# Input projection of a hybrid decoder layer by pairs of column tiles, seven products for eight

## The chip, the core and the metric

The kernel runs on one core of a Trainium2 chip. The metric is the device time of one execution in microseconds (us); lower is better. The engines are PE (TensorE: matmuls), DVE (VectorE), ACT (ScalarE), POOL (GpSimd) and SP, which here only issues DMAs. Each engine runs its own instructions in order, and semaphores order the engines against each other.

## The reference

One step of a one-layer decoder trunk on 512 prompt positions and 64 sample positions (8 sequences of 8), model width 2048. The 576 positions are the moving columns of every large matmul.

```python
h = rmsnorm(x, norm_mix_g)
p = h @ w_in                        # 2048 x 5120: [u_A | v_A | B_gate | C_gate | x_B], 1024 columns each
u = gelu(p[..., :o1])
v = rmsnorm(gelu(p[..., o1:o2]), sgu_norm_g)
bg, cg, xb = p[..., o2:o3], p[..., o3:o4], p[..., o4:]
y_a = u * chunk_sgu(v, w_s, b_s)    # per head: causal 128x128 mixing of positions, plus a bias
zc, new_mix = causal_dwconv(cg * xb, mix_prev, conv_mix_w, conv_mix_b)   # 3 taps
y_b = bg * zc
y = concat(group_rmsnorm(y_a, ..., 8), group_rmsnorm(y_b, ..., 8))       # 16 heads of 128 channels
x = x + y @ w_out
h = rmsnorm(x, norm_ffn_g)
gate, new_ffn = causal_dwconv(h @ w_gate, ffn_prev, ...)
x = x + (silu(gate) * (h @ w_up)) @ w_down
y_out = rmsnorm(x, final_norm_g)
```

## The kernel before

**Data and products.** Everything is held transposed: channels on the 128 partitions, the 576 positions along the free dimension, in two halves of 288 (`HALF`). Float32 accuracy comes from splitting each operand into a high and a low float32r part and making three matmuls: `hi*hi`, `hi*lo`, `lo*hi` (`three`, L1980 to L1982). ACT makes the high part of a weight piece (`w_hi`, L801), DVE subtracts to make the low part (`w_lo`, L1317). A piece is 128x1024 values, half of the rows of one 128-column tile, loaded by SP into one of the two buffers of `raw`. Four pieces fit in `w_hi` and `w_lo`.

**Input projection.** `w_in` has 40 column tiles. One tile is `gemm`: 16 row blocks x 3 matmuls x 2 halves = 96 matmuls of 128x128 by 128x288. The first two tiles run together with the start of the program; the others follow in loops: 8 tiles of v, 8 of u, then 8 times x, C gate, B gate (`group_b`).

**Start.** SP loads x in five blocks (`x_nat`: four of 128 positions, one of 64). PE transposes four 128x128 blocks at a time against the identity (a unit; L2045), DVE multiplies a unit by the norm's gain (L1354), ACT makes `h_hi` (L838) and keeps a copy in `X` (L853), DVE makes `h_lo` (L1343). The norm's own factor is not known yet: the squares are summed beside the first matmuls (ACT L844, DVE L1366), their inverse roots are spread over the partitions by PE (L2059), and every tile of the projection is multiplied by them as it leaves PSUM (`times_rb`, L1326).

**Heads.** While PE runs the u tiles, v is normalised, transposed and mixed per head. Each of the 16 heads of y is squared, split, summed over its 128 channels by PE (`y_ssq`, with a 128x128 block of ones), rooted by ACT (L828), inverted by DVE (L1331, 128x576) and multiplied in place in `X`, one head after the other between the tiles.

**Output projection and the rest.** The first two tiles of `w_out` run row block by row block as the heads of y are ready (`gemm2_by_k`); the residual x comes back from DRAM (`xT_scratch`) by four DMAs of POOL (L623). From the feed-forward part on, pairs of column tiles are made in seven products for eight (Strassen's scheme in Winograd's form: 168 matmuls of 288 columns for 192), with DVE forming sums of weight quadrants (L1685 to L1698) and ACT and DVE combining the results out of PSUM. ACT and DVE run ahead of PE by a four-slot ring of `w_hi` and `w_lo`: piece q may be split once product q-4 is done.

## Time and profile before

| | us |
|---|---|
| median of 3 runs (lowest to highest) | 2291.45 (2290.77 to 2295.84) |
| span of the profiled execution, first to last instruction | 2290.3 |
| PE busy | 2255.6 (98%) |
| DVE busy | 1670.7 (73%) |
| ACT busy | 1021.1 (45%) |
| POOL busy | 498.6 (22%) |
| granted TensorE clock, mean of the span | 0.996 |

Only the span is recorded of the profiled execution, no time of its own; the median of the runs is 1.15 us above it. Busy time of PE counts matmuls whose spans overlap, so that its rate is better read from counts of matmuls over a stretch.

### The profile page before, as it was taken

The page shows a single profiled execution, that of the slowest core. Times are in us where ns is not written, and L with a number is a line of the kernel's source. Part 1 is how long each engine was busy: PE and PEld are TensorE (multiplying, and loading weights), DVE is VectorE, ACT ScalarE, POOL GpSimd, SP SyncE. Part 2 cuts the span into 40 slices and gives each one's busy share as a digit, 9 for nine tenths or more (in the row PEclk, how much of TensorE's full clock was granted, in tenths as well). Part 3 has the DMA queues.
Part 4 walks back from the last instruction along what each step waited for, and adds up shares of the span by engine and source line. Part 5 has one row for each costly group of instructions (what it writes and reads, how often), then busy time and mean ns, then how long its engine had stood idle before and what let it go on. Part 6 is the DMA issues. An engine that isn't in the chain of part 4 may idle for free.

```text
span 2290.3 us, 44103 instructions
## 1 busy us (share of the span) xinstructions
PE 2255.6 (98%) x16946; PEld 2244.7 (98%) x16946; DVE 1670.7 (73%) x2265; ACT 1021.1 (45%) x1608; POOL 498.6 (22%) x593
## 2 busy tenths in 40 slices
PE   7999999999999999999999999999999999999997
PEld 7999999999999999999999999999999999999997
DVE  6347754545522698888888888888888798888886
ACT  6234321212211355455454444545444565555565
POOL 2310000000222011111111111111112356655573
PEclk9999999999999999999999999999999999999998
DMA  7322222232533245454444435344445566765433
GB/s 244 98 76 75 75 82 86 73 92 83 187 101 110 71 116 156 128 163 127 144 140 136 150 121 166 125 146 138 138 150 209 194 228 220 232 228 193 168 113 110
DMA packets 369510, 320.05 MB, mean 140 GB/s; under 512 B 8712, under 2 KB 348803, under 8 KB 364160
## 3 DMA queue, kind: packets, MB, share of 16 engines
q1 hardware_dynamic: 346608, 203.98, 30.5%
q0 software_dynamic: 22800, 114.69, 13.6%
q8 instruction: 66, 1.08, 0.2%
q14 instruction: 36, 0.29, 0.0%
HBM read 258.32 MB, written 60.31 MB: 139 GB/s over the span
## 4 chain that ended last, share of the span: by engine, by line
PE 59%; DMA 1%; DVE 1%; POOL 0%; issue 0%; ACT 0%; POOLq 0%; ACTq 0%
PE ps L2301 13%; PE ps L2303 13%; PE ps L2302 13%; PE ps L2362 6%; PE ps L2364 6%; PE ps L2363 6%; DMA down<-in_w_down_dram 1%; DMA form<-act_scratch 1%; PE ps L2376 0%; DVE dw_lo L1828 0%; DVE w_lo L1672 0%; PE ps L2420 0%; PE ps L2422 0%; PE ps L2421 0%; POOL down_s L714 0%
## 5 line engine op out<-in xcount | busy, mean ns | idle before, releaser
L1980 PE MATMUL ps<-h_hi,w_hi 128*128 128x288 f32 x1728 | 512.9, 297 | 0.0
L1982 PE MATMUL ps<-h_hi,w_lo 128*128 128x288 f32 x1728 | 509.2, 295 | 0.0
L1981 PE MATMUL ps<-h_lo,w_hi 128*128 128x288 f32 x1728 | 509.1, 295 | 0.0
L2362 PE MATMUL ps<-form,dw_hi 128*128 128x288 f32 x1204 | 357.3, 297 | 4.2 <-issue 1.7
L2363 PE MATMUL ps<-form,dw_hi 128*128 128x288 f32 x1204 | 354.3, 294 | 0.0
L2364 PE MATMUL ps<-form,dw_lo 128*128 128x288 f32 x1204 | 353.8, 294 | 0.0
L1980 PEld LDWEIGHTS ps<-h_hi,w_hi 128*128 128x128 f32 x1728 | 324.5, 188 | 0.8
L1981 PEld LDWEIGHTS ps<-h_lo,w_hi 128*128 128x128 f32 x1728 | 324.5, 188 | 0.1
L1982 PEld LDWEIGHTS ps<-h_hi,w_lo 128*128 128x128 f32 x1728 | 324.4, 188 | 0.0
L2301 PE MATMUL ps<-hq,w_hi 128*128 128x288 f32 x1008 | 298.0, 296 | 1.1 <-DVE w_lo L1672 1.1
L2302 PE MATMUL ps<-hq,w_hi 128*128 128x288 f32 x1008 | 296.7, 294 | 0.0
L2303 PE MATMUL ps<-hq,w_lo 128*128 128x288 f32 x1008 | 296.1, 294 | 0.0
L1828 DVE TENSOR_TENSOR dw_lo<-down,dw_hi 128x512 fp32r<-128x512 f32 (+1 forms) x280 | 239.1, 859 | 71.8 <-ACT dw_hi L817 71.3
L1317 DVE TENSOR_TENSOR w_lo<-raw,w_hi 128x1024 fp32r<-128x1024 f32 x120 | 153.4, 1306 | 181.3 <-ACT w_hi L801 181.2
L2362 PEld LDWEIGHTS ps<-form,dw_hi 128*128 128x128 f32 x1204 | 225.7, 187 | 5.8 <-issue 5.3
L2363 PEld LDWEIGHTS ps<-form,dw_hi 128*128 128x128 f32 x1204 | 227.5, 189 | 0.0
L2364 PEld LDWEIGHTS ps<-form,dw_lo 128*128 128x128 f32 x1204 | 227.2, 189 | 0.0
L801 ACT ACTIVATE w_hi<-raw 128x1024 fp32r<-128x1024 f32 x120 | 123.8, 1055 | 227.0 <-PE ps L1982 202.2
L1090 ACT ACTIVATE w_hi<-raw 128x1024 fp32r<-128x1024 f32 x168 | 176.7, 1052 | 79.2 <-DMA raw<-in_w_gate_dram 76.3
L1672 DVE TENSOR_TENSOR w_lo<-raw,w_hi 128x1024 fp32r<-128x1024 f32 x168 | 204.5, 1217 | 10.2 <-ACT w_hi L1090 10.2
L817 ACT ACTIVATE dw_hi<-down 128x512 fp32r<-128x512 f32 (+1 forms) x280 | 166.1, 593 | 92.0 <-PE ps L2364 89.1
L2301 PE MATMUL ps<-tq,w_hi 128*128 128x288 f32 x672 | 198.3, 295 | 0.0
(324 smaller groups left out, 5105.0 us busy)
## 6 DMA issues: line engine op xcount, KB each, us to landing
raw<-in_w_gate_dram SPq DMA_DIRECT2D x88, 512.0 KB, 4.5
raw<-in_w_in_dram SPq DMA_DIRECT2D x80, 512.0 KB, 4.2
down<-in_w_down_dram SPq DMA_DIRECT2D x32, 1024.0 KB, 5.3
form<-act_scratch POOLq DMA_DIRECT2D x28, 1152.0 KB, 7.1
act_scratch<-stage POOLq DMA_DIRECT2D x45, 576.0 KB, 4.7
raw_c<-in_w_up_dram SPq DMA_DIRECT2D x42, 512.0 KB, 3.8
raw_d<-in_w_up_dram SPq DMA_DIRECT2D x42, 512.0 KB, 5.0
raw<-in_w_out_dram SPq DMA_DIRECT2D x32, 512.0 KB, 3.8
```

Of the source, the lines that this page charges most:

```text
L1090: a.activation(w_hi[:, c], quad_form(t), ACT.Copy).then_inc(hi_ready, 1)
L1672: v.tensor_tensor(w_lo[:, c], quad_form(t), w_hi[:, c].bitcast(F32), ALU.subtract).then_inc(lo_ready, 1)
L1828: v.tensor_tensor(dw_lo[:, m % 4, 0:n], down_form(m // NQ, m % NQ), dw_hi[:, m % 4, 0:n].bitcast(F32), ALU.subtract).then_inc(lo_ready, 1)
L1980: te.matmul(out, whi, xhi, start=start, stop=False)
L1981: te.matmul(out, whi, xlo, start=False, stop=False)
L1982: return te.matmul(out, wlo, xhi, start=False, stop=stop)
L2301: te.matmul(out, w_hi[:, c, j, :], b_form(t, 0, j), start=start and j == 0, stop=False, skip_group_check=True)
L2302: te.matmul(out, w_hi[:, c, j, :], b_form(t, 1, j), start=False, stop=False, skip_group_check=True)
L2303: last = te.matmul(out, w_lo[:, c, j, :], b_form(t, 0, j), start=False, stop=stop and j == PJ - 1, skip_group_check=True)
L2362: te.matmul(out, dw_hi[:, m % 4, j, :], act_f[:, j, 0, :], start=start and j == 0, stop=False, skip_group_check=True)
L2363: te.matmul(out, dw_hi[:, m % 4, j, :], act_f[:, j, 1, :], start=False, stop=False, skip_group_check=True)
L2364: last = te.matmul(out, dw_lo[:, m % 4, j, :], act_f[:, j, 0, :], start=False, stop=stop and j == n - 1, skip_group_check=True)
```

## The change

- **Start.** The four full blocks of x are squared by ACT first (`x_square`), rooted per block, inverted, and DVE scales the identity by the result (`diag`). PE then makes an ordinary matmul of `x_nat` with `diag` in place of the transposition, so that the result is already normalised. ACT's copy of each unit goes to a four-deep buffer `xh_stage`, from which POOL writes it to DRAM unit by unit, and ACT waits for the write of four units before. `times_rb` of the projection is gone. The residual's original x is restored later by multiplying with the saved root (`rmsb`).
- **Projection.** Four v tiles stay as they were (`PRE = 4`). The other 36 tiles are 18 visits of two tiles and seven products (`WVIS`): four sums of weight quadrants per visit on DVE (`sum1` to `sum4`), forms of the input made once (four differences over a quarter of X, then splits of them), and for each visit three PSUM copies on ACT and two additions on DVE. `win_c` takes one slot of the ring, so that three are left: piece q may be split once product q-3 is done.
- **Heads.** Gelu works in place in a four-head `ring`; v and y go to DRAM and back. The sums of squares of 8, 4, 2 and 2 heads (`BATCHES`) are gathered in one bank by a one-hot matrix, rooted and inverted together, written to DRAM, and read back broadcast over the partitions. For 14 heads POOL loads y, multiplies it by gain and factor, and stores it (`renorm`); the last two (`DIRECT`) are multiplied by DVE. The loops of the projection are written out.
- **Output projection.** It begins with `out_by_k`: the first half of the columns over row blocks 0 to 13, then the second half, then blocks 14 and 15. POOL multiplies the residual (`resid_scale`, 128x2304 at a time). The parameters of the feed-forward part are transposed here instead of in the projection.

```diff
+    PRE = 4
+    WVIS = (w_in.shape[2] // P - PRE) // 2
+    IN_PIECES = 2 * PRE + 7 * WVIS
+    DIRECT = KT - 2
+    BATCHES = ((0, HEADS), (HEADS, 4), (HEADS + 4, 2), (DIRECT, 2))
...
+            def x_square(tb):
+                act.wait_ge(xnat_landed[tb], 16)
+                a.activation(X[:, :, (TB - 1) * P:TB * P], x_nat[tb][:, :].rearrange("p (k c) -> p k c", k=KT),
+                             ACT.Square, accum_out=ssq_nat[:, tb:tb + 1]).then_inc(ssqn_ready, 1)
...
+                if u >= 4:
+                    act.wait_ge(ring_out[u % 4], 16 * (u // 4))
+                a.activation(xh_stage[:, u % 4, 0:4 * n], ps[:, 4 + kq, 0:4 * n], ACT.Copy).then_inc(xT_copied, 1)
...
-                    last = te.transpose(ps[:, 4 + kq, k * n:(k + 1) * n],
-                                        x_nat[tb][0:n, (4 * kq + k) * P:(4 * kq + k + 1) * P], ident[0:n, 0:n])
+                    last = te.matmul(ps[:, 4 + kq, k * n:(k + 1) * n],
+                                     x_nat[tb][0:n, (4 * kq + k) * P:(4 * kq + k + 1) * P], diag[0:n, tb % 2, 0:n],
+                                     start=True, stop=True)
...
+            def win_hi(vi, t):
+                q = wq(vi, t)
+                act.wait_ge(piece_done, q - 2)
...
+                a.activation(w_hi[:, win_slot(q)], win_form(vi, t), ACT.Copy).then_inc(hi_ready, 1)
...
+            def win_product(vi, t, bank, start, stop):
+                q = wq(vi, t)
+                pe.wait_ge(lo_ready, q + 1)
+                c = win_slot(q)
+                out = ps[:, bank, 0:HALF]
+                for j in range(PJ):
+                    te.matmul(out, w_hi[:, c, j, :], win_x(t, 0, j), start=start and j == 0, stop=False, skip_group_check=True)
+                    te.matmul(out, w_hi[:, c, j, :], win_x(t, 1, j), start=False, stop=False, skip_group_check=True)
+                    last = te.matmul(out, w_lo[:, c, j, :], win_x(t, 0, j), start=False, stop=stop and j == PJ - 1,
+                                     skip_group_check=True)
+                last.then_inc(piece_done, 1)
...
+                win_product(vi, 4, bank, False, False)
+                pe.wait_ge(p5_snap, vi + 1)
+                win_product(vi, 5, 2, False, True)
+                pe.wait_ge(win_c22, vi + 1)
+                win_product(vi, 6, bank, False, True)
...
+            def batch_out(n):
+                first, heads = BATCHES[n]
+                pool.wait_ge(rrms_ready, 1 + n + 1)
+                g.dma_start(r_scr[first:first + heads, :], rr[0:heads, :]).then_inc(r_out, 16)
+                pool.wait_ge(r_out, 16 * (n + 1))
...
+            def renorm(k):
+                g.tensor_scalar(ya[:, :], ya[:, :], vecs[:, G_OUT + k:G_OUT + k + 1], None, ALU.mult).then_inc(pool_scaled, 1)
+                g.tensor_tensor(ya[:, :], ya[:, :], ra[:, :], ALU.mult).then_inc(pool_scaled, 1)
+                g.dma_start(y_scr[:, k * T:(k + 1) * T], ya[:, :]).then_inc(yn_out, 16)
...
+            def out_by_k(half, ks):
+                for kk in ks:
+                    for tile in range(2):
+                        last = three(pair(tile, half), w_hi[:, c, k, :], w_lo[:, c, k, :],
+                                     h_hi[:, kk, cols], h_lo[:, kk, cols], kk == 0, kk == KT - 1)
```

**Three places in the order of instructions.** On ACT, at the start of the program, this stood before (each unit is a split into `h_hi` and a copy to `X`; the numbers of buffers are left as printed):

```order
L832 ACT_TABLE_LOAD
L832 ACTIVATE vecs<-ps 128x16
L838 ACTIVATE h_hi<-scaled 128x4x128
L853 ACTIVATE X<-ps 128x4x128
L838 ACTIVATE h_hi<-u_gelu 128x4x128
L853 ACTIVATE X<-ps 128x4x128
```

and this stands there now (`small` holds the sums and roots, `X` takes the squares, which nobody reads):

```order
L1092 ACT_TABLE_LOAD
L1092 ACTIVATE vecs<-ps 128x16
L1099 ACTIVATE X,small<-x_nat_53 128x16x128
L1106 ACT_TABLE_LOAD
L1106 ACTIVATE small<-small 128x1
L1114 ACTIVATE h_hi<-X 128x4x128
L1117 ACTIVATE xh_stage<-ps 128x512
L1114 ACTIVATE h_hi<-X 128x4x128
L1117 ACTIVATE xh_stage<-ps 128x512
L1099 ACTIVATE X,small<-x_nat_54 128x16x128
L1106 ACTIVATE small<-small 128x1
```

A square of a whole block, a table load and a root now stand ahead of the first unit, and a square and a root ahead of each further block.

On DVE, between the last unit of x and the weights of the third tile, this stood before (sums of squares, then the tiles leave PSUM):

```order
L1366 ISA x_nat_126,small<-x_nat_126 64x2048
L1366 ISA small 64x1
L1368 COPY sel<-ident 128x64
L1372 RECIPROCAL small<-small 128x5
L1376 TENSOR_SCALAR sq<-ident,small 128x128 x4
L1376 TENSOR_SCALAR sq<-ident,small 64x64
L1326 TENSOR_TENSOR scaled<-ps,rb 128x288
L1327 TENSOR_TENSOR scaled<-ps,rb 128x288
L1317 TENSOR_TENSOR w_lo<-raw,w_hi 128x1024 x2
```

and this stands there now (the four differences over a quarter of X each, then splits of weights and of the forms):

```order
L1772 COPY sel<-ident 128x64
L1778 TENSOR_TENSOR X<-X 128x8x288
L1780 TENSOR_TENSOR X<-X 128x8x288
L1782 TENSOR_TENSOR X<-X 128x8x288
L1784 TENSOR_TENSOR X<-X 128x8x288
L1747 TENSOR_TENSOR w_lo<-raw,w_hi 128x1024 x2
L1788 TENSOR_TENSOR t4f<-X,t4f 128x2304
L1747 TENSOR_TENSOR w_lo<-raw,w_hi 128x1024
L1788 TENSOR_TENSOR Xr<-X,Xr 128x8x288
L1747 TENSOR_TENSOR w_lo<-raw,w_hi 128x1024
```

On POOL, beside the first two tiles of the output projection, there were only the four loads of the residual and a memset:

```order
L604 COPY mix_rows<-zpad 128x16
L617 REGISTER_ALU
L617 COMPARE_AND_BRANCH
L623 DMA X<-xT_scratch 128x2304 x4
L626 MEMSET acc 128x576
```

and now (`rr`, `r_scratch`: the factors of the last two heads; `ya`, `ra`: their broadcast rows; `rmsb`: the root that restores x):

```order
L852 DMA ffn_nat<-in_conv_ffn_w_dram 44x3x128
L853 DMA ffn_nat<-in_conv_ffn_b_dram 44x128
L854 DMA ffn_nat<-in_state_conv_ffn_dram 44x16x128
L860 DMA X<-xT_scratch 128x2304 x2
L865 TENSOR_TENSOR X<-X,rmsb 128x2304
L860 DMA X<-xT_scratch 128x2304
L760 DMA r_scratch<-rr 2x576
L875 DMA ya<-r_scratch 128x576
L875 DMA ra<-r_scratch 128x576
L865 TENSOR_TENSOR X<-X,rmsb 128x2304 x2
```

The factors of the last two heads pass through three DMAs, which stand behind a multiplication of a quarter of X and ahead of two more.

## Rows read from the trace of the kernel before

**Rows 1.** The page: busy time, share of the span and instructions of each engine.
```profile
PE 2255.6 (98%) x16946; PEld 2244.7 (98%) x16946; DVE 1670.7 (73%) x2265; ACT 1021.1 (45%) x1608; POOL 498.6 (22%) x593
```

**Rows 2.** Waits of PE, 0 to 900 us: total, times, longest (us).
```profile
PE ps L2045 <- ACT X L853: 6.3, 8, 2.1
PE ps L2045 <- DMA x_nat<-in_x_prompt_dram: 3.5, 1, 3.5
...
PE ps L2137 <- DVE sq_lo L1417: 0.2, 1, 0.2
```

**Rows 3.** Windows: the input projection, then 200 us of feed-forward. PE, PEld, DVE, ACT, POOL.
```profile
25.85:568.40 542.55, 542.55 (x4081) 538.36 (x4080) 292.93 (x343) 156.11 (x203) 42.68 (x60) 1.00 0.31 90
...
1070.00:1270.00 200.00, 200.00 (x1509) 200.00 (x1508) 170.28 (x223) 99.16 (x135) 22.87 (x46) 1.00 0.45 140
```

**Rows 4.** Timeline of PE, 0 to 62 us: start, duration, what.
```profile
6.42 4.85 PE L2045 MATMUL ps<-ident,x_nat 128*128 128x128 f32 x24 [3.48 <-DMA x_nat<-in_x_prompt_dram]
...
25.85 0.59 PE L1980 MATMUL ps<-h_hi,w_hi 128*128 128x288 f32 x1
...
33.12 1.21 PE L2045 MATMUL ps<-ident,x_nat 64*128 64x64 f32 x16
...
50.28 1.05 PE L2059 MATMUL ps<-sq,ones_r 128*128 128x128 f32 x8
...
51.63 0.40 PE L1980 MATMUL ps<-h_hi,w_hi 128*128 128x288 f32 x1
```

**Rows 5.** Timeline of ACT, 0 to 62 us.
```profile
8.98 0.58 ACT L853 ACTIVATE X<-ps 128x512 f32<-128x512 f32 x1
9.46 0.62 ACT L838 ACTIVATE h_hi<-u_gelu 128x512 fp32r<-128x512 f32 x1
...
33.21 1.90 ACT L844 ACTIVATE x_nat<-x_nat 128x2048 f32<-128x2048 f32 x1
35.02 0.19 ACT L844 ACTIVATION_READ_ACCUMULATOR x_nat<-x_nat 128x1 f32 x1
...
44.26 1.28 ACT L872 ACT_TABLE_LOAD   x1 [2.79 <-DVE small L1366]
45.56 0.30 ACT L872 ACTIVATE small<-small 128x5 f32<-128x5 f32 x1
```

**Rows 6.** Groups by line: busy us, mean ns; ACT and DVE, 0 to 850 us.
```profile
L801 ACT ACTIVATE w_hi<-raw 128x1024 fp32r<-128x1024 f32 x120 | 123.8, 1055 | 227.0 <-PE ps L1982 202.2 <-DMA raw<-in_w_in_dram 15.2 <-DMA raw<-in_w_out_dram 7.9
...
L1317 DVE TENSOR_TENSOR w_lo<-raw,w_hi 128x1024 fp32r<-128x1024 f32 x120 | 153.4, 1306 | 181.3 <-ACT w_hi L801 181.2
L1331 DVE RECIPROCAL rms<-rms 128x576 f32<-128x576 f32 x16 | 59.9, 3745 | 0.0
...
L1326 DVE TENSOR_TENSOR scaled<-ps,rb 128x288 f32<-128x288 f32 x24 | 10.9, 456 | 95.5 <-PE ps L1982 89.5 <-ACT rb L877 5.3 <-ACT X L881 0.7
L1663 DVE TENSOR_TENSOR X<-X 128x1152 f32<-128x1152 f32 x8 | 10.4, 1352 | 0.0
```

**Rows 7.** Timelines of POOL and of DVE, 594 to 602 us.
```profile
596.23 1.14 POOL L570 TENSOR_TENSOR psq<-X 128x576 f32 x1 [7.09 <-DVE X L1573]
...
596.23 2.22 DVE L1317 TENSOR_TENSOR w_lo<-raw,w_hi 128x1024 fp32r<-128x1024 f32 x1 [0.21 <-ACT w_hi L801]
```

**Rows 8.** DMA issues: KB each, median us from issue to landing.
```profile
X<-xT_scratch POOLq DMA_DIRECT2D x4, 1152.0 KB, 5.6
act_scratch<-stage POOLq DMA_DIRECT2D x22, 288.0 KB, 2.4
out_dram<-v_nat POOLq DMA_DIRECT2D x8, 32.0 KB, 1.8
vec_nat<-in_norm_ffn_g_dram POOLq DMA_DIRECT2D x1, 8.0 KB, 5.9
raw<-in_w_in_dram SPq DMA_DIRECT2D x80, 512.0 KB, 4.2
```

**Rows 9.** Waits of PE, 840 to 1560 us: total, times, longest.
```profile
PE ps L2301 <- DVE w_lo L1672: 1.1, 2, 0.5
```

More of the change, by code:

```diff
@@ L1377, in _ @@
[L1377 to L1392 removed]
+            every = slice(0, PJ)
@@ L1395, in _ @@
+            form_lo(xqr(every, 0, 0), xq(every, 0, 0), xqr(every, 1, 0), 2)
+            pre_lo(7)
             dve.wait_ge(corner_done, 1)
@@ L2129, in mix @@
                           start=True, stop=True).then_inc(mix_done, 1)
             def y_ssq(n):
[L2133 to L2138 removed]
+                batch = max(b for b in range(len(BATCHES)) if BATCHES[b][0] <= n)
```

1533 lines of the change are left out of this document (984 added, 549 removed).

## The prediction

> **What bounds the kernel now.** I read the busy times first: PE 2255.6 of 2290.3 us, DVE 73%, ACT 45% [rows 1]. Then PE's waits up to 900 us: ten of the few microseconds lie in the transpositions of x, and in the whole input projection there is one of 0.2 us [rows 2]. Then the windows: from the first matmul of the projection (25.85) to the first of the output projection (568.40) PE is busy all 542.55 us, DVE 293 of them and ACT 156. In the feed-forward part PE completes 1509 matmuls in 200 us, 0.1325 us each, at the full granted clock [rows 3]. PE is the bound, so a matmul of 288 columns left out is worth 0.1325 us, as long as the weights still come in time. Every stall that the new scheme makes counts in full too, since PE catches nothing up.
>
> **Products.** 36 tiles at 96 matmuls are 3456; 18 visits of 7 x 24 are 3024. 432 fewer at 0.1325 us: **-57.2 us**. The spreading of the inverse roots goes (50.28 to 51.63, -1.35 us [rows 4]), but the sixteen 64-column transpositions between the first tiles (1.21 us [rows 4]) become float32 matmuls: L2059 shows two records for each of its four 128x128 products, 1.05 us in all, 0.26 each [rows 4]; I take +1.0. Together **-0.3**. The transpositions of the feed-forward parameters only move. Multiplications in `times_rb` and the inversions (3.745 us each, one per head [rows 6]) leave DVE, which is off the path: nothing.
>
> **Start: +9.5.** Before, PE starts to transpose at 6.42, when x has landed, and to multiply at 25.85 [rows 4]. Now a square (1.90 + 0.19), a table load (1.28) and a root (0.30) [rows 5] come first, then an inversion and the diagonal on DVE (about 0.6 with the hand-overs, an estimate from the 0.2 to 0.3 us of small instructions): 4.3 us. Then, for each of the three blocks that the first half of columns needs, ACT has four units of two passes at a pitch of about 0.52 us (8.98 to 9.46 [rows 5]), 4.2 us, and a square and a root more, 2.4: 6.6 us per block, where the old pace was about 4.8. Three blocks, two weight splits of 1.0 [rows 6], and the last block's matmuls on PE bring the first product to 10.8 + 1.0 + 19.8 + 2.0 + 1.7 = 35.3, 9.5 us later. Two things could move it. A small POOL load took 5.9 us while x was loading [rows 8], and `xh_stage` lets four units pass per write: (5.9 + 0.55 for the issue + 0.6 for the copy) / 4 = 1.76 us a unit against 1.65, so it hardly binds at 5.9, and costs 8 us more if a write takes 9. And the first 24 transpositions took 0.20 us each [rows 4]; their successors take about twice that until the granted clock rises: 1.6 us a unit, no slower than ACT. Bounds 6 and 17.
>
> **First visits: +7.** The four differences are 2304 values each, two times L1663's 1.35 us [rows 6]: 10.8 us. They lie beside the first two tiles, which still run 12.8 us in their second half; so far nothing. At visit 0 the queue of DVE is full: after the end of the last plain tile (t = 0) it has a half split of a form until 0.6, w_lo 3.0, another half form 4.4, a sum 5.6; ACT's split 6.8, w_lo 7.9, where product 2 wants it at 6.4: 1.5 us. Then ACT copies a whole form (2.3 us) ahead of the split for product 3, and DVE splits the form (2.7) ahead of w_lo: ready at 13.3 for a product due at 11.1: 2 us. With POOL's additions between them, 4 us. At visit 2 the inversion of v's norm (3.745 us [rows 6]), behind a table load of 1.28 on ACT, stands ahead of the addition and the sum that product 1 of visit 3 needs: ready 11.6 us after product 4, wanted at 9.6, and 1 us for what follows: 3 us. Bounds 2 and 12.
>
> **The steady visits: +3.** A visit takes PE 168 x 0.1325 = 22.3 us. DVE has seven w_lo and four sums at about 1.17 us of pitch, 12.9, two additions, 0.9, and up to 6 of head work: 14 to 20 us. ACT has 7 x 1.055 and six or so short copies: 11 to 15. Both fit. With three slots, a piece may be split when product q-3 ends and is wanted two products later, 6.4 us; split and w_lo take 1.055 + 1.22, so 4.1 us remain for what stands ahead of them in the two queues. Behind product 5 stand an addition, a sum, w_lo, a low square, the gating, the v norm and the next sum: by the same durations the piece for product 2 is ready 10.5 us later and wanted at 10.9. It fits, barely. The nearest row is the feed-forward part, the same scheme with four slots and more DVE work (170 of 200 us [rows 3]): 1.1 us of waiting in 720 us, 32 pairs [rows 9]. From below the cost is nothing; from above, one slot less takes 3.2 us of slack from each visit, and if half of that showed up it would be 1.6 x 18 = 29. I take 3 (the inversion of the first batch ahead of the last addition of visit 9 is 1 of it), near the feed-forward row.
>
> A POOL multiplication slows DVE: a w_lo beside `psq` took 2.22 us for 1.22 [rows 7], and the mean of w_lo is 1.306 [rows 6]. The 28 POOL passes of `renorm` add up to 1.1 us each, 31 us of DVE over nine visits with 200 us of PE; where the slack is 0.4 to 2 us some will show. The Trainium skill (SBUF — State Buffer, SBUF: two separate sides) says that the port pair which DVE and GpSimd share is an exclusive lock, held for a whole instruction by either. Row and rule agree for one pass of 1.14 us; taken literally for all 28 on the path it would add 31 us, against my 3 by the feed-forward row.
>
> **The first tiles of w_out: +9.** (a) Product 5 of the last visit ends at -3.2, product 6 at 0. DVE then has an addition, two multiplications, w_lo (-1.0), three low parts of y (1.3) and w_lo of the second tile (2.5), which PE wants at 0.4: 2.2 us. (b) Heads 14 and 15. PE sums head 15 at about 16.5 and would want row block 14 at 26.1. The root is done at 17.4, the inversion of a 2-row batch takes the same 3.745 us [rows 6], since it goes by columns: 21.3. The store takes 1.8 to 2.4 us, the broadcast load 2.4 [rows 8], with issues of 0.55: 27.7. Two multiplications, a high and a low part: 30.2, 4.1 us late. (c) By then POOL is in a multiplication of 2304 columns, four times `psq`'s 1.14, 4.6 us, and another follows; if DVE waits as in [rows 7], 2 to 7 us more, of which I take 3. Sum 9.3, taken as 9; bounds 2 and 16. The residual's scaling needs 4 x 4.6 us and has 50 us before the fourth tile: nothing.
>
> **Sum.** 2290.3 - 57.2 - 0.3 + 9.5 + 7 + 3 + 9 = 2261.3 of span; plus the 1.15 by which the runs' median stands above this span: **2262 us**, 1.3% faster.
>
> **The rivals.**
> 1. *As forecast*, half of the saving given back at both ends: 2262, its own range 2253 to 2271. Chance 0.52.
> 2. *The ends hide better.* PE's clock rises earlier, ACT's squares overlap, the factors come with no contention: start 6, first visits 2, steady 1, end 4. 2290.3 - 57.5 + 13 + 1.15 = 2247. For it: the old start has idle time on every engine; against it: the queues as counted. Chance 0.16 (2240 to 2253).
> 3. *The three-slot ring leaks.* 1 us in each of 18 visits beyond the 3, from the slack of 0.4 to 2 us and POOL's passes: 2262 + 18 = 2280. For it: rows 7; against it: rows 9. Chance 0.22 (2271 to 2287).
> 4. *Slower.* The same place and no other: DVE late for product 2 of every visit. The gain left is 29 us; over 18 visits the decision falls at 1.6 us more per visit. At 2.2 us more it is 2262 + 40 = 2302. The lock taken literally (31 us) gives 2293, which is no change. For it: one slot less is worth 3.2 us. Against: DVE is idle 2 to 8 us per visit and would have to be late in spite of it. Chance 0.06, and 0.04 for no change.
>
> That the change does nothing is excluded: 432 matmuls of the bound engine are gone.
>
> A measurement of this kernel can tell about 0.2%, 4.6 us. Faster takes cases 1 to 3, 0.90; the same 0.04; slower 0.06. Range: from case 2 to the top of case 3, 2246 to 2282.
>
> **What the profile after will show.** PE's first 288-column product near 35 us (step *Start* is right if between 32 and 38); PE busy and its matmul count down by 432; waits of PE on DVE's w_lo at visit 0 and at visit 3, and otherwise under 5 us from there to the last visit; visits of 22.3 us, 27.5 where heads are mixed. At the boundary one wait of about 2 us on w_lo, and one of 5 to 10 us on DVE's low part of head 14, behind a DMA of `r_scratch`; DVE instructions of double length beside POOL's 4.6 us multiplications. The feed-forward part should be the same to 1 us. The forecast is wrong if PE waits in every visit, if the writes of `xh_stage` take over 9 us, or if the two late heads cost over 16.

## The result, and the profile after the change

The changed kernel takes 2310.52 us (median of 4 runs, 2304.64 to 2315.24), the kernel before 2291.3 beside it: ratio 1.0076, 95% interval 1.0056 to 1.0095. It is **0.8% slower**; 2262 was forecast, with a range up to 2282. The profiled execution was the fastest of the four, 2304.64 us with a span of 2302.8.

The page of the changed kernel: span, busy times, and the row of granted clock (40 slices of the span, tenths of full speed).

```profile
span 2302.8 us, 43217 instructions
## 1 busy us (share of the span) xinstructions
PE 2222.2 (96%) x16584; PEld 2206.3 (96%) x16584; DVE 1765.3 (77%) x2315; ACT 1104.2 (48%) x1747; POOL 648.9 (28%) x730
...
PE   6999999998799999999999999999999999999997
...
PEclk9999999998899999999999999999999999999998
```

Against [rows 1], PE has 362 matmul records fewer and is busy 33 us less, though the span is 12.5 us longer: the work is gone, and more than that came back as time in which PE stands still or runs slowly. The waits of PE (in all, times, longest) from 0 to 900 us say where; [rows 2] had ten of the few microseconds at the start and 0.2 in the projection:

```profile
PE ps L2631 <- DVE w_lo L1807: 15.0, 13, 2.2
PE ps L2524 <- issue: 12.4, 3, 5.3
PE ps L2491 <- DVE h_lo L2079: 12.3, 1, 12.3
PE ps L2524 <- DVE diag L1742: 7.8, 1, 7.8
PE ps L2491 <- DVE w_lo L1968: 6.9, 2, 5.0
PE ps L2604 <- DVE sq_lo L1841: 4.8, 3, 2.3
```

L2631 is a product of a visit, L2524 the transposition of x, L2491 a plain product (here of the output projection), L2604 the sum of squares of a head. I cut the span where these stages meet. The windows of the changed kernel: first product to the last visit's end, from there to the feed-forward part, and the rest (columns as in [rows 3]):

```profile
45.63:559.22 513.59, 493.62 (x3633) 482.18 (x3631) 368.49 (x375) 220.40 (x315) 158.50 (x172) 0.99 0.46 133
559.22:792.08 232.86, 213.57 (x1573) 211.66 (x1572) 89.21 (x103) 53.27 (x66) 72.28 (x59) 0.95 0.41 127
792.08:2302.78 1510.70, 1492.34 (x11255) 1490.36 (x11253) 1284.42 (x1798) 801.29 (x1321) 403.21 (x466) 1.00 0.49 158
```

| stage | before | after | change | forecast |
|---|---|---|---|---|
| start, to the first 288-column product | 25.85 | 45.63 | +19.8 | +9.5 |
| input projection | 542.55 | 513.59 | -29.0 | -57.5 + 7 + 3 |
| output projection, to the feed-forward part | 206.88 | 232.86 | +26.0 | +9 |
| feed-forward part to the end | 1515.04 | 1510.70 | -4.3 | 0 |

In later profiles of the changed kernel and its variants the last row lies between 1512.7 and 1516.5, as before: the 4.3 us belong to this one execution. Of the +26.0 of the output projection, 1.9 us are work of PE that the change moves there from the row above it: 1.4 for the transpositions of the feed-forward parameters and 0.5 for the sum of squares of one more head. Three things are in the other rows.

**The start.** Times of ACT, DVE and PE for one block of x (start, duration, engine, line; in brackets the idle time ahead and who ended it):

```profile
16.33 1.90 ACT L1099 ACTIVATE X<-x_nat 128x2048 f32<-128x2048 f32 x1
...
18.36 0.29 ACT L1106 ACTIVATE small<-small 128x1 f32<-128x1 f32 x1
18.56 0.61 ACT L1114 ACTIVATE h_hi<-X 128x512 fp32r<-128x512 f32 x1
...
19.20 0.69 DVE L1733 TENSOR_TENSOR h_lo<-X,h_hi 128x512 fp32r<-128x512 f32 x1 [1.01 <-ACT h_hi L1114]
...
19.81 0.15 DVE L1738 RECIPROCAL small<-small 128x1 f32<-128x1 f32 x1
...
20.39 5.17 PE L2524 MATMUL ps<-diag,x_nat 128*128 128x128 f32 x32 [3.10 <-issue]
...
23.20 0.63 ACT L1114 ACTIVATE h_hi<-X 128x512 fp32r<-128x512 f32 x1 [2.54 <-DVE X L1759]
```

The square of block 1 (L1099) runs only at 16.33, behind two units of block 0; its diagonal waits on DVE for one more low part; then PE starts, and ACT idles 2.54 us until PE's first unit has passed DVE. PE, DVE and ACT work one after the other. The blocks start at 10.81, 20.39, 29.62 and 40.54: a pitch of 9.2 to 9.6 us, and 10.9 with two splits of weights. And there are four of them: PE's program has block 3 ahead of the first product.

**The visits.** PE's matmuls of the projection are all in the trace, so each visit can be timed (us, visits 0 to 17, start to start):

```
after    26.61 23.70 24.65 28.93 27.70 27.71 27.70 23.54 22.28 23.81 23.32 23.05 29.18 22.28 24.05 28.90 23.70 26.26
```

Two reach 22.28, the rate of the products. What the others wait for is best seen at visit 12. DVE, ACT and POOL in the hand-over from visit 11:

```profile
400.13 1.06 ACT L1168 ACTIVATE w_hi<-raw 128x1024 fp32r<-128x1024 f32 x1 [3.64 <-DMA raw<-in_w_in_dram]
...
400.97 1.42 POOL L776 TENSOR_TENSOR ya<-ya,ra 128x576 f32<-128x576 f32 x1
...
401.23 2.25 DVE L1807 TENSOR_TENSOR w_lo<-raw,w_hi 128x1024 fp32r<-128x1024 f32 x1 [0.95 <-ACT w_hi L1168]
403.51 1.22 DVE L1814 TENSOR_TENSOR raw<-raw,win_c 128x1024 f32<-128x1024 f32 x1
404.65 0.45 DVE L1964 TENSOR_TENSOR half_sum<-ps,snapu 128x288 f32<-128x288 f32 x1
405.14 0.39 DVE L1932 TENSOR_TENSOR ring<-half_sum,cb 128x224 f32<-128x224 f32 x1
405.45 0.22 DVE L1933 TENSOR_TENSOR ring<-half_sum,cb 128x64 f32<-128x64 f32 x1
405.58 1.22 DVE L1820 TENSOR_TENSOR win_c<-win_c,win_d 128x1024 f32<-128x1024 f32 x1
...
407.17 1.06 ACT L1168 ACTIVATE w_hi<-win_c 128x1024 fp32r<-128x1024 f32 x1 [5.98 <-DVE win_c L1820]
...
408.26 1.23 DVE L1807 TENSOR_TENSOR w_lo<-win_c,w_hi 128x1024 fp32r<-128x1024 f32 x1 [1.46 <-ACT w_hi L1168]
...
409.77 1.22 DVE L1826 TENSOR_TENSOR win_c<-win_d,raw 128x1024 f32<-128x1024 f32 x1
```

This is one serial chain: the load lands, the piece for product 0 is split on ACT and DVE, then `sum3` in place, then `sum1` in place, split again for product 1 (PE starts it at 409.64, 1.6 us late), then `sum2` in the same buffer `win_c`, split again for product 2. ACT waits for DVE (5.98 us) and DVE for ACT in turn. From product 1 to product 2 the chain takes 3.9 us (1.2 + 1.1 + 1.2 and hand-overs) for a product of 3.2. The chain also starts late: ACT stood still for 3.64 us until the piece for product 0 had landed. A POOL multiplication beside the first split made 2.25 us of its 1.22.

**The output projection.** Its first product waits 5.0 us for the first low part, a second wait for a low part is 2.0 us, and heads 14 and 15 cost one wait of 12.3 us. POOL and DVE at that place:

```profile
588.47 0.53 POOL L760 DMA_DIRECT2D r_scratch<-rr  x1 [1.66 <-DVE rr L1884]
592.20 0.56 POOL L875 DMA_DIRECT2D ya<-r_scratch  x1 [3.20 <-DMA r_scratch<-rr]
592.75 0.54 POOL L875 DMA_DIRECT2D ra<-r_scratch  x1
593.30 10.03 POOL L865 TENSOR_TENSOR X<-X,rmsb 128x2304 f32<-128x2304 f32 x2
...
598.23 5.73 DVE L2075 SCALAR_TENSOR_TENSOR X<-ring,vecs,ya 128x576 f32<-128x576 f32 x1 [6.77 <-DMA ra<-r_scratch]
603.88 0.81 DVE L2075 SCALAR_TENSOR_TENSOR X<-ring,vecs,ra 128x576 f32<-128x576 f32 x1
```

Store and load take 3.7 and about 5.5 us; then head 14's multiplication, 0.8 us of work as its twin shows, ends at 603.96, 0.6 us behind the end of POOL's second 5.0 us multiplication (603.33). Behind these waits the clock is low. Windows of the changed kernel behind the wait of 2.0 us and behind that of 12.3 (the figure ahead of the last two is the granted clock):

```profile
567.00:573.00 6.00, 5.61 (x24) 5.61 (x25) 2.54 (x5) 2.27 (x4) 0.00 (x0) 0.52 0.54 141
...
605.50:610.00 4.50, 4.48 (x18) 4.48 (x19) 0.69 (x1) 0.00 (x0) 0.57 (x1) 0.50 0.48 150
```

0.50 is the lower of the two levels, 1.2 GHz: matmuls of 288 columns come every 0.24 us there instead of 0.1325. Summed over all such stretches: 5.6 us in the visits and 4.7 in the output projection, against 1.1 in the same stages before.

### The profile page after: what moved, and what is told of

The parts are those of the page before. It is cut to its first block, busy times and chain, and to the rows that moved or that the text cites. A ratio compares the mean times of both kernels' runs of the same rounds, so it can differ in the third digit from the quotient of the medians.

```text
span 2302.8 us, 43217 instructions
## 1 busy us (share of the span) xinstructions
PE 2222.2 (96%) x16584; PEld 2206.3 (96%) x16584; DVE 1765.3 (77%) x2315; ACT 1104.2 (48%) x1747; POOL 648.9 (28%) x730
## 4 chain that ended last, share of the span: by engine, by line
PE 60%; DMA 1%; DVE 1%; POOL 1%; issue 0%; ACT 0%; POOLq 0%; ACTq 0%
PE ps L2826 13%; PE ps L2828 13%; PE ps L2827 13%; PE ps L2887 6%; PE ps L2889 6%; PE ps L2888 6%; DMA form<-act_scratch 1%; PE ps L2901 0%; DVE w_lo L2183 0%; PE ps L2945 0%; PE ps L2947 0%; PE ps L2946 0%; POOL X L989 0%; POOL down L983 0%; POOL down_s L982 0%
## 5 line engine op out<-in xcount | busy, mean ns | idle before, releaser
L913 POOL DMA_DIRECT2D act_scratch<-stage x67 | 44.6, 666 | 657.4 <-DVE stage L2151 634.0
L2491 PE MATMUL ps<-h_hi,w_hi 128*128 128x288 f32 x640 | 192.1, 300 | 19.3 <-DVE h_lo L2079 12.3
L1484 ACT ACTIVATE w_hi<-raw 128x1024 fp32r<-128x1024 f32 x168 | 176.8, 1052 | 69.5 <-DMA raw<-in_w_gate_dram 67.3
L2183 DVE TENSOR_TENSOR w_lo<-raw,w_hi 128x1024 fp32r<-128x1024 f32 x168 | 204.6, 1218 | 5.0 <-ACT w_hi L1484 4.8
L2826 PE MATMUL ps<-tq,w_hi 128*128 128x288 f32 x672 | 198.3, 295 | 0.0
L2827 PE MATMUL ps<-tq,w_hi 128*128 128x288 f32 x672 | 198.2, 295 | 0.0
L2826 PE MATMUL ps<-Xr,w_hi 128*128 128x288 f32 x672 | 198.0, 295 | 0.0
L2828 PE MATMUL ps<-tq,w_lo 128*128 128x288 f32 x672 | 198.0, 295 | 0.0
L2828 PE MATMUL ps<-Xr,w_lo 128*128 128x288 f32 x672 | 197.8, 294 | 0.0
L2827 PE MATMUL ps<-Xr,w_hi 128*128 128x288 f32 x672 | 197.7, 294 | 0.0
L2493 PE MATMUL ps<-h_hi,w_lo 128*128 128x288 f32 x640 | 190.6, 298 | 0.0
```

The source lines that it names most:

```text
L1484: a.activation(w_hi[:, c], quad_form(t), ACT.Copy).then_inc(hi_ready, 1)
L2183: v.tensor_tensor(w_lo[:, c], quad_form(t), w_hi[:, c].bitcast(F32), ALU.subtract).then_inc(lo_ready, 1)
L2491: te.matmul(out, whi, xhi, start=start, stop=False)
L2493: return te.matmul(out, wlo, xhi, start=False, stop=stop)
L2826: te.matmul(out, w_hi[:, c, j, :], b_form(t, 0, j), start=start and j == 0, stop=False, skip_group_check=True)
L2827: te.matmul(out, w_hi[:, c, j, :], b_form(t, 1, j), start=False, stop=False, skip_group_check=True)
```

## Experiments

Sixteen kernels ran. The theory: the forecast's steps are right in kind, and three orders of work make them too small (start, sum chain, small neighbours of heads 14 and 15). The rival is that of the prediction: three slots, and POOL's passes on a shared port. "Visits 9 to 17" is the time from the first matmul of visit 9 to the end of 17; nine visits of 22.28 are 200.5, and with the 3.6 us of sums of squares that PE makes in visits 9, 12 and 15 they are 204.1 without any wait. Waits are the idle time in the trace, as in the rows above. e3 to e10, e12 and e13 were timed once each, and the changed kernel's own times spread over 11 us, so I go by stages.

**e0_again**: no edit.

> The changed kernel once more, unchanged. Its four timed runs lay between 2304.64 and 2315.24 us, and the profiled one was the fastest of them. If the loss is in waits whose length is set by orders in the queues, the start (first product of 288 columns at 45.6 us) and the wait for heads 14 and 15 (12.6 us) come out again within 0.5 us, and what varies lies in the waits of the visits, which depend on when weights land. If these two waits were chance, they move by several us.

2316.31 us (4 runs, 2311.31 to 2318.36; ratio to before 1.0097, 1.0076 to 1.0118). First product at 46.38, the waits at the output projection 6.7, 5.3 and 10.6 us (5.0, 2.0 and 12.3 in the first profile), visits 9 to 17 226.08 against 224.55. The start moved by 0.75 and the late heads' wait by 1.8 us, more than the 0.5 I expected, but not by several. 4 us of the difference are the feed-forward part, and 3.1 lie ahead of the visits, where part of the first tiles ran at a granted clock of 0.80. The visits start at 101.9 or 102.0 in two of the profiles with an unchanged start, and at 104.8 to 106.7 in the others.

**e1_start**
```diff
-                    if kq == 1 and tb < TB:
-                        x_square(tb + 1)      # ScalarE
+                if tb < TB:
+                    x_square(tb + 1)
...
-                    if kq == 3 and tb < TB:
+                    if kq == 0 and tb < TB:   # VectorE: x_diag(tb + 1)
...
-            for tb in range(TB):
+            for tb in range(3):               # PE
                 x_transposes(tb)
-                    if half == 0 and tile == 0:
-                        x_transposes(TB)
+                        elif tile == 0:
+                            x_transposes(3 + s)
```


> Two changes of order at the start: ScalarE squares block tb+1 before the units of block tb (and VectorE makes its diagonal after the first of them), and PE transposes block 3 between the first products instead of ahead of them. Theory (the chain of square, root and diagonal stood behind two units of the block before, and a fourth block stood ahead of the products): the pitch of the blocks falls from 9.2 to 9.6 us to about 6.6, the first product comes at 34 to 37 us instead of 45.6, and the run is 8 to 11 us shorter. Rival (ScalarE's work and the writes of the staging ring bound the start): the pitch stays above 9 us, the first product comes no earlier than 38, the second half of columns waits for blocks 3 and 4, and the run is less than 4 us shorter.

First product at 37.1, 9.3 us before that of the control; the blocks start at 10.85, 16.48 and 22.24, a pitch of 5.6 to 5.8 us. But the visits start at 102.35 (control 105.66, profile after 101.85). Of the 9.3 us, block 3 takes 3.5 on PE now behind the first product, and slow matmuls take most of the rest. Windows of this run, in the wait ahead of the first product, from that product on, and behind the transpositions of block 4:

```profile
27.00:37.00 10.00, 0.18 (x2) 0.00 (x0) 6.96 (x11) 7.38 (x13) 2.25 (x3) 0.75 0.59 153
37.10:42.30 5.20, 5.20 (x21) 5.20 (x22) 2.45 (x2) 4.19 (x7) 0.75 (x1) 0.50 0.85 263
53.80:59.40 5.60, 5.60 (x24) 5.57 (x24) 5.28 (x6) 0.69 (x2) 4.77 (x8) 0.50 0.54 80
```

The order was the cause of the late first product, as the theory has it. What it bought at the start of the visits is 3.3 us against the control and nothing against the first profile, so a gain is not shown: 2312.87 us (2305.76 to 2315.84).

**e2_resid**: POOL's order behind the second half of the heads' loads.
```diff
             resid_load(0)
-            resid_load(1)
             resid_scale(0)
-            resid_load(2)
+            resid_load(1)
             batch_out(3)
             ...
-            resid_scale(1)
-            resid_scale(2)
+            resid_load(2)
             resid_load(3)
-            resid_scale(3)
+            for s in range(1, 4):
+                resid_scale(s)
```


> GpSimd scales rows 4 to 15 of the residual, and loads rows 8 to 15 of it, only after the two late heads: its order is changed, no work is left out. Theory (the 12.6 us wait for heads 14 and 15 is made by GpSimd's own neighbours: 1.15 MB in its queue ahead of the small loads, and two multiplications of 5 us during which VectorE's first product of head 14 takes 5.7 us for 0.8): that product takes 0.8 us, the two loads land in 2 to 4 us, the wait falls to 3 to 6 us, and the run is 7 to 11 us shorter. Rival (root, inversion, store and load are long by themselves): the wait stays above 9 us, and the run is at most 4 us shorter.

```profile
603.78 0.82 DVE L2074 SCALAR_TENSOR_TENSOR X<-ring,vecs,ya 128x576 f32<-128x576 f32 x1 [7.18 <-DMA ra<-r_scratch]
```

Head 14's multiplication takes 0.82 us instead of 5.73: its length was POOL's. The wait falls to 7.9 us, between theory and rival, since the load still takes 5.0 us and the store 4.1. Output projection 228.9 us against 232.9 and 235.7; the whole 2313.07 (2308.55 to 2315.34), within the spread of the unedited kernel.

**e4_filler**
```diff
             out_by_k(1, range(2, DIRECT))
+            for n in range(96):
+                te.matmul(ps[:, T_BANK, 0:HALF], w_hi[:, 2, n % 6, :], h_hi[:, n % DIRECT, 0:HALF], start=True, stop=True)
```


> Ninety-six matmuls of 288 columns that nobody reads are put in front of the products of heads 14 and 15, where PE waits 12.6 us; they write a PSUM bank that is free. They add work and take none away. Theory (the slow matmuls behind a wait come from the wait itself): the filler fills 12.7 us, the matmuls behind it come every 0.13 us at once instead of 18 of them at 0.24, and the feed-forward part starts 1 to 2 us earlier in spite of the added work. Rival (the clock falls at this place for another reason, such as the work before it): the matmuls behind the filler are as slow as before, and the feed-forward part starts at the same time or later.

The filler takes 12.5 us, then a window of the products of heads 14 and 15:

```profile
610.00:613.00 3.00, 3.00 (x25) 3.00 (x24) 0.13 (x1) 0.00 (x0) 0.57 (x1) 1.00 0.44 104
```

The 24 matmuls of half 0 take 3.18 us instead of 5.45 (and 5.81 in e0_again), and from the first of them to the feed-forward part it is 184.3 us instead of 186.6 and 186.9. At this place the low clock comes from the wait; work that nobody needs is worth 2.3 us there. The single time of the run, 2312.68 us, doesn't show it.

**e3_short**: in `renorm`, both multiplications on `ya[:, 0:1]`.

> The 28 multiplications of GpSimd in renorm work on one column instead of 576, so that heads 0 to 13 reach the output projection without their norm and gain: work is left out, all loads, stores and waits stay. Theory (most waits of the visits come from the serial chain of the weight sums, which share one buffer, and GpSimd only adds to it): in visits 9 to 17 the waits and slow matmuls fall from 22 us to between 10 and 16, and waits ahead of products 1 and 2 stay. Rival 3 of the prediction (GpSimd's passes on the port that VectorE shares make the waits): in visits 9 to 17 they fall below 5 us.

2298.04 us. Visits 9 to 17: 212.5, which is 8.4 us above 204.1, for 20.4 in the first profile and 22.0 in e0_again. That lies between the theory (10 to 16) and the rival (under 5): the passes of POOL are worth 12 to 14 us, more than half of what is lost there, and w_lo waits stay. A thing that neither foresaw: the first pieces of w_out now land in 3.9 to 6.9 us (4.6 to 13.7 in e0_again); PE waits 1.3 us ahead of the first product instead of 6.7, and 4.0 instead of 5.3 behind it. The likely reason is that POOL is through earlier with `renorm` and the heads' loads are more out of their way. It is argued, not shown: in the profiles with `renorm` and the sums at full length the first of these waits lies between 2.5 and 6.7 us and the second between 2.0 and 6.6.

**e5_yload**
```diff
                 pool.wait_ge(piece_done, wq(WVIS - 1, 4 if half else 1) + 1)
+                if half:
+                    pool.wait_ge(hi_ready, IN_PIECES + 2)
```


> The two loads of the heads' second half of columns from y_scratch are issued only when ScalarE has split the second piece of w_out, some 9 us later. Theory (4 MB of heads beside the first two pieces of w_out make these land in 9.0 us): the pieces land in 4 to 6 us, the first product of w_out starts 3 to 5 us earlier and the wait behind it falls from 2.4 to under 1.5 us; the second halves of the heads are still in time. Rival (VectorE's queue, with four low parts ahead of the split, makes the wait): w_out starts less than 1.5 us earlier.

Refuted: the wait ahead of the first product is 4.8 us and the next 2.0, as in the first profile, and two new waits (2.7 and 2.0) stand before the second half. 2319.13 us, the longest of all. The half that I left in place was issued at 550.35, behind `renorm` of head 13, and that is still beside the first piece. That POOL's lateness makes these landings long fits e3_short, but no run shows it by itself.

**e6_ssq**: `y_ssq` of visits 9, 12, 15 behind products 2 and 4 instead of 1 and 3.

> In visits 9, 12 and 15 PE takes the sums of squares of the two heads before one product later each (behind product 2 and product 4). Theory (each of these three waited for the low square, 0.5 to 2.6 us, and at visits 12 and 15 the clock fell behind the wait): 5 us of waits and 2.5 us of slow matmuls go, the visits together are 5 to 8 us shorter. Rival (the wait only moves to the next sum of weights, which is late by as much): the visits are less than 2 us shorter.

Visits together 459.95 us against 459.18. Visit 12 fell by 2.9 and visit 13 grew by 2.6. 2313.44 us. The rival holds: without slack in the chain a wait only moves.

**e7_order**
```diff
                     win_lo(vi + 1, 0)
                     sum3(vi + 1)
+                    sum1(vi + 1)
...
-                    sum1(vi + 1)
+                    if kind in "cg":
+                        take_c21(vi)
                     win_lo(vi + 1, 1)
```


> On VectorE the sum of weights for product 1 of the next visit stands directly behind the one for product 3, ahead of the head's additions and multiplications (0.45 to 1.06 us), and the last quarter of a visit (0.45 us) goes ahead of the split for product 1. Theory (the chain piece 0, sum, sum, split, product 1, sum, split, product 2 is serial and 0.1 to 0.3 us short of its time in every visit that waits): the waits ahead of products 1 and 2 fall by 0.5 to 1.1 us each, together by 8 to 12 us over the visits. Rival (the landing of the weights decides): the waits shrink by less than 3 us, since the chain starts as late as before.

The visits take 453.02 us against 459.18: 6.2 us, between the two (visits 9 to 17 alone 223.6 for 226.1); the run 2313.56. The chain is where it was said to be, but hiding 1 us of it per visit isn't enough.

**e8_gain**
```diff
+                if n < DIRECT:                # ScalarE, in y_square
+                    a.activation(ring[:, n % 4, :], ring[:, n % 4, :], ACT.Copy,
+                                 scale=vecs[:, G_OUT + n:G_OUT + n + 1]).then_inc(y_gained, 1)
```


> ScalarE multiplies a head by its gain behind its square, before it is stored, so that GpSimd makes one multiplication per head in renorm instead of two; no work is left out. Theory (GpSimd's passes make some 13 us of waits in visits 9 to 17, by the run with passes of one column, and end so late that the heads' loads run beside the first pieces of w_out): half of that comes back, visits 9 to 17 take 217 to 221 us instead of 224.5 to 226, and the run is 6 to 10 us shorter. Rival (what counts is only whether a pass overlaps a split, and one pass overlaps as often as two): visits 9 to 17 stay above 223 us.

Visits 9 to 17: 217.9, as the theory has it. But visits 4 to 6 grew from 27.7 to 32.4, 31.6 and 29.7: there POOL stores a head before it loads the next of v, and the store now waits for the gain. 2314.51 us.

**e9_bcast**: e2_resid, and
```diff
+            for n in range(2):                # PE, ahead of kk = 12 of the second half
+                for half in range(2):
+                    last = te.matmul(ps[:, 4 + 2 * n + half, 0:HALF], ya[0:2, n * P:(n + 1) * P],
+                                     rr[0:2, half * HALF:(half + 1) * HALF], start=True, stop=True)
+                last.then_inc(r_bc, 1)
```


> The inverse norms of heads 14 and 15 no longer go through DRAM (a store and two broadcast loads); four matmuls of two rows spread them over the partitions, and VectorE reads them from PSUM; GpSimd's scaling of rows 4 to 15 stands behind the two heads as in the second run. Theory (what is left of the wait is the store of 4 us and the loads of 5 us beside 512 KB pieces of w_out): the two heads are ready 8 to 10 us earlier, the wait falls from 8 to under 2 us, no slow matmuls follow, and the output projection is 9 to 12 us shorter than in the kernel after the change. Rival (the inversion of 3.7 us and the root come too late by themselves): a wait of 4 us or more stays.

The products of heads 14 and 15 follow the others without a gap (603.83, 603.96), at full clock. The output projection takes 225.1 us, 7.7 and 10.6 less than in the two profiles of the changed kernel. 2303.57 us.

**e10_start**: e1_start with `x_transposes` of blocks 3 and 4 cut into units between products, and
```diff
+            pe.wait_ge(xhi_ready, 8)
+            for n in range(56):
+                te.matmul(ps[:, 3, 0:2 * P], h_hi[:, n % KT, 0:P], h_hi[:, n % KT, 0:2 * P], start=True, stop=True)
```


> As the first run of the start, but blocks 3 and 4 are transposed unit by unit between the products of the first half, and 56 matmuls of 256 columns that nobody reads fill PE's wait of 10 us ahead of the first product. Theory (the first run gave back 6 of its 9 us in slow matmuls behind that wait and behind the transpositions of block 4): the first product comes at 36 to 38 us, no product runs at 0.24 us, and the visits start at 93 to 97 us instead of 102 to 106. Rival (the time went into waits for blocks 3 and 4, not into the clock): slow matmuls go but waits of 4 us or more come between the products, and the visits start later than 99 us.

First product at 37.6, visits at 100.03, 5.6 us before the control and 1.8 before the first profile; slow matmuls 1.1 us, waits 0.3. I expected 93 to 97 and had not counted the 3.5 us of block 3 on PE. 2314.57 us: the rest of this one execution was longer.

**e11_all**: e7 to e10 together.

> All of it together: the start with filler and spread transpositions, the order of sums on VectorE, the gain on ScalarE, the residual's scaling behind the two late heads, their inverse norms spread by PE. By the parts: start 8 to 10 us, visits 10 to 14, w_out's first pieces 2 to 5, late heads 9 to 12, from about 2312: 2272 to 2284, faster than the kernel before (2292). Rival (waits only move from one serial chain to the next, as the run with the sums of squares showed): 2288 to 2300, no better than before.

2280.73 us (6 runs, 2278.72 to 2283.86), ratio to before 0.9946 (0.9934 to 0.9958): 0.5% faster than the kernel before and in the range summed from the parts.

**e12_sums, e13_sums_short**: the four sums on `[..., 0, 0:8]`; and with e3_short's passes too.

> The four sums and differences of weights of each visit work on 8 columns instead of 1024: their waits stay, the weights of products 1, 2, 3 and 5 are wrong, so work is left out. GpSimd's passes are as in the kernel after the change. Theory (a wait needs both: the serial chain through the one buffer of the sums, and GpSimd's passes on top of it): with the chain 1.2 us shorter per sum, visits 9 to 17 fall from 224.5 to 226 us to 203 to 210, and visits 0 to 3 from 104 to under 100. Rival (GpSimd's passes and the late landing of weights make the waits whatever the sums cost): visits 9 to 17 stay above 215.

> Both left out: the sums of weights work on 8 columns, GpSimd's multiplications in renorm on one. Theory: visits 9 to 17 take 200.5 to 203 us, at or near nine visits of 22.28, and what stays is the wait for the low square of a head. Rival (a third cause, the landing of weights or the ring of three slots): 206 us or more.

```
                 visits 0 to 17                                                                                             9-17
after            26.61 23.70 24.65 28.93 27.70 27.71 27.70 23.54 22.28 23.81 23.32 23.05 29.18 22.28 24.05 28.90 23.70 26.26  224.6
e3_short         26.61 22.73 24.44 29.90 27.71 27.71 27.69 23.53 22.28 23.81 22.73 22.28 26.07 22.28 22.28 25.10 22.62 25.34  212.5
e12_sums         24.48 22.28 23.36 27.30 27.48 27.48 27.49 23.49 22.28 23.47 22.28 22.28 23.50 22.28 22.28 23.47 22.28 22.28  204.1
e13_sums_short   24.50 22.28 23.36 27.30 27.48 27.48 27.49 23.49 22.28 23.47 22.28 22.28 23.50 22.28 22.28 23.47 22.28 22.28  204.1
```

With the sums short the visits are the same with POOL's passes and without them, to 0.03 us, and PE has no wait in visits 9 to 17. So in the visits neither POOL's passes nor the three slots cost anything by themselves; POOL's 12 to 14 us are there only because the chain of sums has no slack. Short sums take away all of the loss of visits 9 to 17, short passes 60% of it: the chain makes 40% alone, and 60% needs both. Nearly all of the steady visits' loss lies where POOL works beside the chain: of the 21.1 us that visits 4 to 17 lose against e12, 20.4 are in visits 9 to 17. What is above 200.5 is PE's own work, 1.2 us of sums of squares in each of visits 9, 12 and 15.

Two rivals stay open. The short sums also take 32 us off DVE in visits 9 to 17 (131.9 us busy for 164.1), so that the one shared buffer isn't told apart from the mere length of DVE's queue; for the chain speak DVE's 27% of idle time there in the changed kernel and e7_order. And ACT's waits for the landing of weights in these visits fall from 18.8 us in six places to 7.5 in two; no run changed the landings alone, nor gave a fourth slot with the sums at full length.

The time doesn't go away with the visits. e12 has another wait instead (in all, times, longest):

```profile
PE ps L2491 <- DVE w_lo L1968: 18.1, 2, 16.1
```

The visits are done, and POOL's `renorm` of 14 heads, one load, two passes and one store after the other, is not: by itself it is nearly as long as visits 9 to 17. With its passes short (e13) that wait is 2.4 us at most. So POOL's passes, free in the visits of e12, cost it 14.0 us of waiting here, and the whole is 2297.56 us for e12 and 2279.03 for e13. The wait for heads 14 and 15 stays, 13.1 and 12.2 us.

**e14_best, e15_ssq**: e11_all, with `v_load(p + 2)` ahead of `y_spill(p)`; and that with e6_ssq.

> All of the eleventh run together, and GpSimd loads the next head of v ahead of storing the head that waits for its gain. Theory (visits 4 to 6 grew from 27.7 to 28.4 us with the gain on ScalarE, since the loads of v stood behind the later stores): they return to 27.5, and the run takes 2277 to 2279 us against 2280.7. Rival (ScalarE's added passes make visits 4 to 6 longer): no change from 2280.7.

> As the run beside it, and the sums of squares in visits 9, 12 and 15 stand one product later on PE. Alone on the changed kernel this moved the waits and gained nothing. Theory (there was no slack then; now there is): visits 12 and 15 fall by 1.5 us each, and the run is 2 to 4 us shorter than the one beside it. Rival (the wait moves again to the next product): the same time within 1 us.

e14: 2275.87 us (5 runs, 2270.69 to 2278.83), ratio to before 0.9916 (0.9898 to 0.9934), the best; visits 4 to 6 are back at 27.5. e15: 2279.03 (2277.28 to 2280.23), no gain: visits 12 and 14 change by -1.2 and +1.2 us, the wait moves again. Windows of e14, visits and output projection:

```profile
98.33:540.81 442.48, 430.99 (x3206) 421.71 (x3204) 336.31 (x347) 208.40 (x297) 107.74 (x135) 1.00 0.47 138
540.81:759.90 219.09, 212.87 (x1580) 210.12 (x1579) 91.28 (x103) 51.66 (x63) 70.79 (x56) 0.98 0.43 131
```

## Why the prediction was wrong

The saving was right: 432 matmuls went, and with the sums short the visits run at 22.28 us. PE's records are down 362, not 432, since each of the 80 transpositions of x leaves two as a float32 matmul (and ten for the inverse roots went). The sixteen of 64 columns went from 1.2 to 3.7 us, where +1.0 was taken. Three of the four terms against the saving were too small, and together they turned the sign.

**Start, +9.5, measured +19.8.** The failed step is "for each of the three blocks ... 6.6 us per block": ACT's passes were added up as if ACT were always busy. PE, DVE and ACT alternate, so the pitch is 9.2 to 9.6 (some 7 of the 10.3 us missed), and PE's own order has a fourth block, 5.1 us, ahead of the product where 1.7 was counted (the other 3.4). The bound of 17 was too low. That `xh_stage` doesn't bind held: in e1_start two blocks followed each other without a wait for a write.

**First visits, +7, measured +8.5** (visits 0 to 3, against 22.28 three times, 27.5, and the 1.0 us of v's sum of squares in visit 2): right. Visit 0 costs 4.3 us for 4, and product 1 of visit 3 waits 1.85 us behind the inversion of v's norm, where 2 of the 3 were put; 1.4 us at visit 1 were not forecast.

**Steady visits, +3, measured +21** (visits 4 to 17 against e12_sums). This is the step that failed most in its reasoning. "It fits, barely" was worked out for one piece and its slot. The chain through the shared buffer (split, sum, sum, split, sum, split) was not followed from the landing of the weights to product 2. In 11 of the 18 visits product 2 starts 0.15 to 0.18 us after its low part is done, so nothing is left to give; and "the nearest row is the feed-forward part" misled: [rows 9] come from a scheme whose sums go to a buffer of their own, `raw_e` (that this makes the difference is argued, no run tried it). Rival 3 had a size near the measured one (18 us more) and half of the cause: POOL's passes are 12 to 14 us of it on top of a chain without slack, while e12 and e13 show no cost of the three slots once the sums are short.

**First tiles of w_out, +9, measured +26.** Counted by how late a matmul starts, 0.2 to 0.3 us more than the idle time ahead of it: (a) 2.2 us were 7.4 (5.1 and 2.3): the two first pieces landed in 9.0 us beside the heads' loads, and a landing was not in the sum. (b) and (c), 4.1 and 3, were 12.5: the store took 3.7 us and the load 5.5 where 1.8 to 2.4 was taken from [rows 8], though the same rows have 5.9 for a small load of POOL; and (c) 4.9 of "2 to 7", of which I took 3. The mechanisms of (b) and (c) are shown by e9 and e2. Their order in time is as forecast. Slow matmuls add 4.2, and 1.9 is work moved from the projection.

**Missing altogether: the clock behind a wait.** 10.3 us of slow matmuls in the two stages, against 1.1 before. Each wait was priced at its length; in the first profile another 1.2 to 2.3 us followed behind each wait of 2.0 us or more (the two at the start of w_out, three matmuls apart, counted as one). e4_filler shows it for the longest. For the short ones it goes by the execution: behind the wait of 2.0 us in visit 0 and the two of 2.3 us at the sums of squares 14, 12 and 11 matmuls were slow in the first profile, and none behind the same three in e9_bcast.

**The rivals.** Slower had 0.06, by 2.2 us more in every visit. It came in another way: 10 + 18 + 17 us at three places, none of which would have decided alone. The terms were taken as independent, each near the lower half of its bounds; the sum of the upper bounds (17, 12, 29, 16) would have been 2308, still under the measured 2310.52. The range of 2246 to 2282 was also narrower than its own cases 1 to 3, which run from 2240 to 2287. That rival 3's size comes near the measured one is luck: it took 1 us in each of 18 visits, and the loss is in nine.

**The port.** The Trainium skill (SBUF — State Buffer, SBUF: two separate sides) has a VectorE instruction with two SBUF inputs fully blocked while a GpSimd instruction that reads SBUF is under way, and the other way round. The trace agrees: head 14's multiplication took 5.73 us for 0.82, from 598.23 to just behind POOL's instruction, and a low part of weights took 6.05 for 1.2 beside another of 5.15. In e9_bcast, where POOL makes three such multiplications in a row (605.54 to 620.93), a low part begun at 608.58 took 13.44 us, while the four additions just before it, with one operand in PSUM, took their usual 0.45 each. The reciprocal, which has one input, took its usual 3.74 beside such a multiplication (584.43, POOL's from 581.12). Taken literally for all passes the rule gave +31 for the visits; measured are 12 to 14 in visits 9 to 17, and none there when the chain has slack.

## What to carry to other kernels

When a product's operand is made by sums in one shared buffer, write the chain out from the landing of the load to the last product that hangs on it, with every engine's turn in it, and compare that with the products between: adding up each engine's busy time shows slack where there is none. Before costing a GpSimd pass or an edit of a queue at nothing, ask whether the chain beside it has slack, and what waits for GpSimd's last pass: the same passes cost 12 to 14 us in the visits, or nothing there and 14 us of waiting at the next stage. And price a wait of PE of more than 4 us at its length and 1 to 2 us more, or fill it: small trips through DRAM (10 us for two rows) are better made by PE itself when it would stand still anyway.

## What was unexpected of the hardware

- Behind a wait of 12.3 us (and of 9.9 in e1_start) the matmuls of 288 columns ran at 0.24 us for 4.5 to 5.2 us (granted clock 0.50, the 1.2 GHz level), and after 12.5 us of filler in place of the 12.3 at 0.1325 from the first.
- It also fell without a long wait: behind 4.2 to 4.4 us of 64-column transpositions, 5.5 us at 0.50 in e1_start and 0.80 over 50 to 60 us in e0_again, where the first profile kept full clock behind the same transpositions, made there in 3.7 us.
- A VectorE instruction with two operands in SBUF stood for the whole of two more GpSimd instructions behind the one under way: 13.44 us for 1.2.
- A store of 4.6 KB took 3.7 to 4.1 us to land, and a broadcast load of 288 KB 5.0 to 5.5, beside loads of 0.5 to 1.2 MB. That these neighbours made them long is argued; no run took them all away (in e2_resid one 1.2 MB load still stands right ahead of the store).
